# The mLSTM stabiliser as a prefix scan over rows of keys, one spread per head, and one branch product in another bank

## The reference, cut to what matters

```python
b = jnp.cumsum(fc, axis=-1)
log_d = jnp.where(causal, b[..., :, None] - b[..., None, :] + ic[..., None, :], -jnp.inf)
m_inter = b + m_prev[..., None]
m_t = jnp.maximum(m_inter, jnp.max(log_d, axis=-1))
a = jnp.exp(m_inter - m_t)
s_qk = jnp.einsum("bhtd,bhsd->bhts", qc, kc) * jnp.exp(log_d - m_t[..., None])
...
h = num / jnp.maximum(jnp.abs(den), jnp.exp(-m_t))[..., None]
...
mix = jax.nn.sigmoid(gm) * (y_m @ w_br_mlstm[l]) + jax.nn.sigmoid(gf) * (y_f @ w_br_fox[l])
```

## Time and profile before

| | us |
|---|---|
| median of 3 runs | 794.84 (794.53 to 795.08) |
| the profiled execution's own time | 794.99 |
| its span in the trace | 793.1 |
| TensorE busy | 778.2 (98%) |
| VectorE busy | 373.1 (47%) |
| ScalarE busy | 254.6 (32%) |
| GpSimd busy | 25.4 (3%) |

### The profile page before, as it was taken

One profiled execution on the slowest core, in us unless ns is written; L12 is line 12 of the kernel. 1 busy time (PEld: TensorE's weight loads), 2 busy tenths in 40 slices (PEclk: granted clock), 3 DMA queues, 4 the chain that ended last, 5 costly groups with the idle time before them and its releaser, 6 DMA issues.

```text
span 793.1 us, 9542 instructions
## 1 busy us (share of the span) xinstructions
PE 778.2 (98%) x3851; PEld 639.7 (81%) x3851; DVE 373.1 (47%) x576; ACT 254.6 (32%) x421; POOL 25.4 (3%) x45
## 2 busy tenths in 40 slices
PE   6999999999999999999999999999999999999996
PEld 6988888788666688888889888888888888888885
DVE  4688434356877444252446443343344444223224
ACT  6444221244455232322333322232233233123111
POOL 5000000012100000000000000000000000000000
PEclk9999999999999999999999999999999999999999
DMA  7434333211111035322421333233333223322302
GB/s 228 126 100 141 124 107 106 58 50 54 54 54 47 8 107 192 104 76 105 140 73 54 107 107 90 73 103 107 106 107 106 69 91 109 124 87 74 139 0 107
DMA packets 61916, 75.64 MB, mean 95 GB/s; under 512 B 3680, under 2 KB 49840, under 8 KB 61872
## 3 DMA queue, kind: packets, MB, share of 16 engines
q1 hardware_dynamic: 61872, 75.02, 29.5%
HBM read 72.92 MB, written 2.10 MB: 95 GB/s over the span
## 4 chain that ended last, share of the span: by engine, by line
PE 71%; issue 1%; DVE 0%; ACT 0%; POOLq 0%; POOL 0%; DVEq 0%; ACTq 0%
PE bank L1146 22%; PE bank L1148 22%; PE bank L1147 22%; PE bank L1367 1%; PE bank L1335 1%; PE bank L1352 1%; PE bank L1158 0%; PE bank L1342 0%; PE bank L1339 0%; ACT square_out L449 0%; DVE probs L978 0%; ACT x L684 0%; DVE yfT_lo L955 0%; DVE work L873 0%; DVE x L1118 0%
## 5 line engine op out<-in xcount | busy, mean ns | idle before, releaser
L1146 PE MATMUL bank<-hT_hi,w_hi 128*128 128x512 f32 (+1 forms) x680 | 261.2, 384 | 2.1 <-DVE hT_lo L709 2.1
L1148 PE MATMUL bank<-hT_hi,w_lo 128*128 128x512 f32 (+1 forms) x680 | 257.2, 378 | 0.0
L1147 PE MATMUL bank<-hT_lo,w_hi 128*128 128x512 f32 (+1 forms) x680 | 257.0, 378 | 0.0
L725 DVE TENSOR_TENSOR w_lo<-stage,w_hi 128x1024 fp32r<-128x1024 f32 x125 | 152.4, 1223 | 221.8 <-ACT w_hi L469 213.2
L469 ACT ACTIVATE w_hi<-stage 128x1024 fp32r<-128x1024 f32 x127 | 133.4, 1053 | 132.0 <-PE bank L1148 127.4
L1146 PEld LDWEIGHTS bank<-hT_hi,w_hi 128*128 128x128 f32 x680 | 128.8, 189 | 26.1 <-POOL w_lo L412 2.3
L1148 PEld LDWEIGHTS bank<-hT_hi,w_lo 128*128 128x128 f32 x680 | 128.7, 189 | 23.8
L1147 PEld LDWEIGHTS bank<-hT_lo,w_hi 128*128 128x128 f32 x680 | 128.8, 189 | 21.7
L1146 PE MATMUL bank<-w_hi,aT_hi 128*128 128x512 f32 x176 | 68.5, 389 | 0.0
L1147 PE MATMUL bank<-w_lo,aT_hi 128*128 128x512 f32 x176 | 68.5, 389 | 0.0
L1148 PE MATMUL bank<-w_hi,aT_lo 128*128 128x512 f32 x176 | 68.5, 389 | 0.0
(11 more groups left out here) (175 smaller groups left out, 765.3 us busy)
## 6 DMA issues: line engine op xcount, KB each, us to landing
stage<-in_w_in SPq DMA_DIRECT2D x21, 1024.0 KB, 5.2
stage<-in_w_gate SPq DMA_DIRECT2D x11, 1024.0 KB, 5.3
stage<-in_w_up SPq DMA_DIRECT2D x11, 1024.0 KB, 5.3
stage<-in_w_down SPq DMA_DIRECT2D x22, 512.0 KB, 4.4
stage<-in_w_out SPq DMA_DIRECT2D x4, 1024.0 KB, 5.0
x_nat<-in_x SPq DMA_DIRECT2D x4, 512.0 KB, 5.7
stage<-in_w_br_mlstm SPq DMA_DIRECT2D x4, 512.0 KB, 3.5
stage<-in_w_br_fox SPq DMA_DIRECT2D x4, 512.0 KB, 4.6
```

Of the source, the lines that this page charges most:

```text
L725: dve.tensor_tensor(ring(w_lo, g), staged(g), ring(w_hi, g).bitcast(F32), ALU.subtract).then_inc(lo_split, 1)
L1146: pe.matmul(o, a_hi, b_hi, start=first, stop=False)
L1147: pe.matmul(o, a_hi, b_lo, start=False, stop=False)
L1148: return pe.matmul(o, a_lo, b_hi, start=False, stop=last)
```

## The change

The four spreads of a key row per head are gone, with the maxima on them. In their place the running maximum is taken where the keys lie as rows: a `tensor_tensor_scan` on VectorE, for each block of queries q, over the (q + 1) x 128 keys of four heads on four partitions, straight from the bank of the transposes, with `before` of the head as start value. The scans run from q = 3 down to 0 and write the same row `m_rows` from its start, so that in the end each block of 128 columns is the one of its own q. For that, `ROW_CHUNKS` now puts all keys of q = 3 in bank 7, of q = 2 in bank 6, and of q = 0 and 1 in bank 5, and `before` is brought to rows by four matmuls with one column of the identity. ScalarE and VectorE write the high and low part as `m_both` (a buffer of 128x512 that GpSimd clears first). After the second granule of `G_FV`, four matmuls turn `m_rows` into columns for `m_floor`. The spread of a head is one fp32r matmul of 512 columns with `pick` as weights. The banks 5 to 7 are now free for the next taker when the scans have read them. The branch products of the mLSTM go to banks 2 and 3, those of FoX to banks 0 and 1.

```diff
+        m_both = at("m_both", [P, SEQ], F32R, R + 77 * K)
+        m_rows = work[0]
...
@@ POOL, among the constants
+            const(pool.memset(m_both[:, :].bitcast(F32), 0.0))
@@ ACT, in the loop over granules
+                if g == G_MV + 3:
+                    act.wait_ge(m_scan, ROWS)
+                    act.activation(m_both[0:H_M, :], m_rows[0:H_M, :], ACT.Copy).then_inc(m_hi_ready, 1)
...
-            act.wait_ge(m_step, 2)
+            act.wait_ge(m_step, 1)
@@ DVE, at g == G_MV + 2, behind the low halves of the keys
+                    dve.wait_ge(frame_T, 1)
+                    dve.tensor_copy(before_rows[:, :], psum[5][0:H_M, BEFORE_AT:BEFORE_AT + ROWS]).then_inc(before_copied, 1)
+                    dve.wait_ge(before_copied, 1)
+                    for i, q in enumerate(reversed(range(ROWS))):
+                        n = next(n for n, (a, b) in enumerate(ROW_CHUNKS) if a <= pair(q, 0) < b)
+                        c = (pair(q, 0) - ROW_CHUNKS[n][0]) * P
+                        if i >= 1:
+                            dve.wait_ge(m_scan, i)
+                        dve.tensor_tensor_scan(m_rows[0:H_M, 0:(q + 1) * P], psum[5 + n][0:H_M, c:c + (q + 1) * P],
+                                               before[0:H_M, 0, 0:1].to_broadcast([H_M, (q + 1) * P]),
+                                               before_rows[:, q:q + 1], ALU.max, ALU.add).then_inc(m_scan, 1)
+                if g == G_MV + 3:
+                    dve.wait_ge(m_hi_ready, 1)
+                    dve.tensor_tensor(m_both[LO:LO + H_M, :], m_rows[0:H_M, :], m_both[0:H_M, :].bitcast(F32),
+                                      ALU.subtract).then_inc(m_lo_ready, 1)
+                if g == G_FV + 2:
+                    dve.wait_ge(m_columns, 1)
+                    dve.tensor_tensor(m_floor[:, :, :], psum[M_COLUMNS_BANK][:, 0:ROWS * H_M].rearrange("p (q h) -> p q h", q=ROWS),
+                                      cum[:, :, 0:H_M], ALU.add).then_inc(m_step, 1)
...
-                if G_FQK <= g < G_MO:
-                    for u in spread_units(g - G_FQK):
-                        q, h = u // H_M, u % H_M
-                        dve.wait_ge(g_spread, u + 1)
-                        dve.reduce_max(m_stab[:, q, h:h + 1], psum[spread_bank(u)][:, 0:(q + 1) * P], AX.X).then_inc(g_max, 1)
...
@@ PE, keys_as_rows
-                    take(5 + n, (rows_lo_ready, n + 1))
+                    take(5 + n, (m_scan, (ROWS, 2, 1)[n]))
+                    if n == 0:
+                        for q in range(ROWS):
+                            pe.matmul(psum[5][0:H_M, BEFORE_AT + q:BEFORE_AT + q + 1], before[:, q, :], ident[:, 0:1],
+                                      start=True, stop=True)
...
+            def stabiliser_columns():
+                pe.wait_ge(m_scan, ROWS)
+                take(M_COLUMNS_BANK, (m_step, 1))
+                for q in range(ROWS):
+                    last = pe.matmul(psum[M_COLUMNS_BANK][:, q * H_M:(q + 1) * H_M], m_rows[0:H_M, q * P:(q + 1) * P],
+                                     ident[0:H_M, 0:H_M], start=True, stop=True)
+                last.then_inc(m_columns, 1)
...
-                for u in spread_units(b):
-                    q, h = u // H_M, u % H_M
-                    take(spread_bank(u), (g_max, u + 1))
-                    spread_row(spread_bank(u), h, q, True, True).then_inc(g_spread, 1)
@@ PE, mlstm_scores
-                    pe.wait_ge(m_step, 2)
+                    pe.wait_ge(m_lo_ready, 1)
...
-                for q in range(ROWS):
-                    last = pe.matmul(psum[2][:, q * P:(q + 1) * P],
-                                     m_stab[:, q, h:h + 1].to_broadcast([P, P]), ident[:, :], start=True, stop=True)
-                last.then_inc(m_spread, 1)
+                pe.matmul(psum[2][:, :], pick[:, h:h + 1].to_broadcast([P, P]), m_both[:, :], start=True,
+                          stop=True).then_inc(m_spread, 1)
@@ PE, the branches
-                    columns(g, 2 * j, (mix_step, 3 * b + 1), ymT_hi, ymT_lo, 0, KB, False)
+                    columns(g, YM_BANKS[j], (mix_step, 3 * b + 1), ymT_hi, ymT_lo, 0, KB, False)
...
-                    columns(g, 2 * j + 1, (mix_step, 3 * b + 2), yfT_hi, yfT_lo, KB, KB)
+                    columns(g, YF_BANKS[j], (mix_step, 3 * b + 2), yfT_hi, yfT_lo, KB, KB)
...
-ROW_CHUNKS = ((0, 4), (4, 8), (8, 10))
+ROW_CHUNKS = ((0, 3), (3, 6), (6, 10))
+BEFORE_AT = 3 * P
+M_COLUMNS_BANK = 4
+YM_BANKS, YF_BANKS = (2, 3), (0, 1)
```

More of the change, by code:

```diff
@@ L231, in block_kernel @@
         before = small("before", [P, ROWS, H_M])
-        m_stab = small("m_stab", [P, ROWS, H_M])
+        before_rows = small("before_rows", [H_M, ROWS])
         m_floor = small("m_floor", [P, ROWS, H_M])
@@ L268, in block_kernel @@
         rows_hi_ready, rows_lo_ready, rows_low_half = sem("rows_hi_ready"), sem("rows_lo_ready"), sem("rows_low_half")
-        g_spread, g_max, m_step, floor_ready = (sem(n) for n in ("g_spread", "g_max", "m_step", "floor_ready"))
+        before_copied, m_scan, m_hi_ready, m_lo_ready = (sem(n) for n in ("before_copied", "m_scan", "m_hi_ready", "m_lo_ready"))
+        m_columns, m_step, floor_ready = (sem(n) for n in ("m_columns", "m_step", "floor_ready"))
         m_spread, s_m, decay_exp, m_masked, weighted = (sem(n) for n in ("m_spread", "s_m", "decay_exp", "m_masked", "weighted"))
@@ L1042, in _ @@
                         s = mix_sum[b % 2]
-                        dve.scalar_tensor_tensor(out=s[:, :], in0=work[2 + j][:, :], scalar=1.0, in1=psum[2 * j][:, :],
+                        dve.scalar_tensor_tensor(out=s[:, :], in0=work[2 + j][:, :], scalar=1.0, in1=psum[YM_BANKS[j]][:, :],
                                                  op0=ALU.add, op1=ALU.mult).then_inc(mix_step, 1)
-                        dve.scalar_tensor_tensor(out=work[0][:, :], in0=work[4 + j][:, :], scalar=1.0, in1=psum[2 * j + 1][:, :],
+                        dve.scalar_tensor_tensor(out=work[0][:, :], in0=work[4 + j][:, :], scalar=1.0, in1=psum[YF_BANKS[j]][:, :],
                                                  op0=ALU.add, op1=ALU.mult).then_inc(mix_step, 1)
@@ L1263, in _ @@
                         keys_as_rows()
-            def spread_row(bank, lane, q, first, last):
-                n = (q + 1) * P
-                cols = slice(pair(q, 0) * P, pair(q, 0) * P + n)
-                both = pick[:, lane:lane + 1].to_broadcast([P, P])
-                pe.matmul(psum[bank][:, 0:n], both, rows_both[:, cols], start=first, stop=False)
-                return pe.matmul(psum[bank][:, q * P:n], ident_b[:, :], mask_b[:, :], start=False, stop=last)
+                    if n == 1 and d == 1:
+                        stabiliser_columns()
             for b in range(8):
                 z_columns(G_FQK + b, fqk_bank(b), (fq_ready, b + 1) if b < KB else (fk_ready, b - KB + 1))
-                if b == 0:
-                    pe.wait_ge(rows_lo_ready, 3)
-                for u in spread_units(b):
-                    q, h = u // H_M, u % H_M
-                    take(spread_bank(u), (g_max, u + 1))
-                    spread_row(spread_bank(u), h, q, True, True).then_inc(g_spread, 1)
             def mlstm_scores(h):
                 if h == 0:
-                    pe.wait_ge(m_step, 2)
+                    pe.wait_ge(m_lo_ready, 1)
                     pe.wait_ge(qk_ready, 8)
                 take(2, (decay_exp, 10 * (h + 1)))
-                for q in range(ROWS):
-                    last = pe.matmul(psum[2][:, q * P:(q + 1) * P],
-                                     m_stab[:, q, h:h + 1].to_broadcast([P, P]), ident[:, :], start=True, stop=True)
-                last.then_inc(m_spread, 1)
+                pe.matmul(psum[2][:, :], pick[:, h:h + 1].to_broadcast([P, P]), m_both[:, :], start=True,
+                          stop=True).then_inc(m_spread, 1)
                 for j in range(ROWS):
```

10 lines of the change are left out of this document (1 added, 9 removed).

## The result

| | before | after |
|---|---|---|
| median, same chip | 794.96 (794.53 to 795.39, 4 runs) | 788.50 (787.94 to 790.44, 4 runs) |
| the profiled execution / its span | 794.99 / 793.1 | 788.84 / 787.0 |

The ratio is 0.9921, with a 95% interval of 0.9909 to 0.9933. The forecast was 787.7 (785.9 to 789.9).

The account below looks back on a forecast made before the run. TensorE, busy 98% of the span, was taken to bound the kernel. Savings of 4.57 + 2.6 + 1.5 = 8.7 us less 1.6 added gave 7.1 off the median 794.84: 787.7 us, range 785.9 to 789.9.

Parts of the forecast that it names:

- Sixteen spreads: TensorE, projections of the FoX q and k: removing 16 spreads and their masks saves 4.57 us, all on the path.
- Small matmuls: TensorE: eight added float32 matmuls, for `before` as rows and the stabiliser's columns, cost 1.6 us together.
- The heads: TensorE, mLSTM heads: one fp32r matmul replaces four float32 spreads in each of four heads, saving 2.6 us.
- nothing new becomes late: Behind each head's spread: mask, exponentials and weighing start from the spread's end, so they add no wait.
- The bank: First branch product with `ymT`: in bank 2 it no longer waits for `yfT_lo`, and the 1.5 us goes whole.
- The scans, hidden: VectorE, after the keys' low halves: four scans, 1.6 us, cost nothing if they end by about 89.3 us.
- The memset, hidden: GpSimd at the start: one more memset of 512 columns, about 0.46 us, hidden by 0.1 us.
- The small matmuls at full price: Rival, TensorE's added matmuls: each record costs its whole length, 3.4 us instead of 1.6, 789.5 us; chance 0.13.
- free: Rival, TensorE's added matmuls: they slip under their neighbours and cost nothing, 786.1 us; chance 0.08.
- The branch's wait: Rival, branch products: the product with `yfT` waits after all or for weights, 1.5 us stays, 789.2 us; chance 0.06.
- The late scans: Rival, bank 5: slow scans make TensorE wait, slower than before from 15.6 us of scans; chance 0.02.
- The change does what it says: Its opposite was a rival, FoX projections: place, not removed matmuls, causes the 4.57 us; 2 us stays, 789.7 us; chance 0.01.

Follow-up runs that it names:

- e5: Changed kernel with the 16 spreads, masks and maxima put back, their results unused: 793.50 us, ratio 0.9976 to the kernel before.
- e6: Changed kernel with the stabiliser's columns made by four transposes instead of four float32 matmuls: 788.32 us, ratio 0.9913 to the kernel before.
- e1: Changed kernel with the next head's mask put ahead of the normalisation on VectorE: 787.56 us, ratio 0.9908 to the kernel before.
- e2: Kernel before with the next head's mask put ahead of the normalisation on VectorE: 795.31 us, ratio 1.000 to the kernel before.
- e4: Changed kernel with each head's stabiliser spread by four float32 matmuls from its columns again: 790.84 us, ratio 0.9948 to the kernel before.
- e3: Kernel before with only the branch products moved to the other banks: 793.74 us, ratio 0.9981 to the kernel before.
- e11: Changed kernel with two more memsets of 512 columns on GpSimd at the start: 789.11 us, one run.
- e7: Changed kernel with each of the four scans done three times: 792.52 us, ratio 0.9969 to the kernel before.
- e8: Changed kernel with early mask, columns by transposes, and head 3's normalising ahead of taking head 2's transposed output: 787.27 us, ratio 0.9901 to the kernel before.
- e9: Changed kernel run again without any edit: 789.11 us, ratio 0.9928 to the kernel before.

## Why the prediction was right, and the step that failed

- **Sixteen spreads, 4.57 us: right.** Shown by e5, 4.57 between two places of its trace. The way to it, the stretch less its projections by the pitch, counts the switches without naming them.
- **Small matmuls, 1.6 us: the sum right, its parts not.** Measured 0.37 for `before` (0.7 taken) and 1.19 for the columns (0.9 taken). The step that failed is one price of 0.085 for both, read off transposes. A record of `before` (four columns of weights, one moving) cost 0.27 / 8 = 0.034 us; one of the columns (128 columns of weights, four moving) cost 0.12, and e6 shows that a transpose of that shape costs 0.08. The errors of +0.3 and -0.3 cancelled, which is luck. The Trainium skill ("TensorE: Matmul & The Clock Gate", section "LDWEIGHTS (loading the stationary operand)") has the load go by the weights' columns alone. The estimate by it, 1.1 us, was closer for the columns than my 0.9, though 0.12 lies a little over its 0.107, and the 0.08 of the transposes below it; for `before` its 0.0 to 0.2 was too low by about as much as my 0.7 was too high.
- **The heads, 2.6 us: right where it was read, and wrong behind it.** By the first FoX logits 2.65 us had come. The failed step is "nothing new becomes late". I had argued that the mask hangs on the spread's end. It hangs on two things, and the other is VectorE's own turn: behind the gate and ScalarE's tanh for head 1, and behind the normalisation and GpSimd's power from then on. The change shortens neither by as much as TensorE's way: 0.03 to 0.37 us a head against 0.66 to 0.69. The trace before had it: head_output ended at 203.80, and the logits that need it started 0.16 us later. With the wait, after, they start 0.14 us behind its end (199.41 to 199.55). So that place had no slack at all. TensorE didn't show a wait there because it came at the same moment. e1, e2 and e4 show the mechanism from three sides: the earlier mask brings 1.2 us after and nothing before, and with slow spreads the wait goes.
- **The bank, 1.5 us: right.** 1.6 in the traces, and e3 alone gives 1.5. The slack of 1.3 us that was worked out for the product with `yfT` held: it starts at 267.51, `yfT_lo` ends at 266.10.
- **The scans, hidden: right, though they were priced at less than half.** Their size hardly mattered since the cover was read off first. The Trainium skill ("DVE: opcode table, instruction layouts, handler registers and perf-mode slots", section "6. Datapath and trigger behaviour") says half throughput for the built-in scan, and the estimate of 3 us by it was near. The trace after agrees: 2.08 ns an element (1.27 us for 512, 0.47 for 128), where the two-input operation that weighs the scores (L921), from PSUM too, takes 0.69 us for 512 elements and 0.28 for 128, 1.07 ns an element.
- **The memset, hidden: right.** 0.52 us, in the idle time that was there; e11 adds that the slack behind is real.
- **The rivals.** None came true. The small matmuls at full price (3.4 us) and free (0) both fall at 1.56. The branch's wait didn't come back. The late scans lost 0 and would begin to lose at 8 us, by e7. The change does what it says, by e5. None of them named VectorE's lag in the heads, which took 1.2 us, more than the error of any term that was priced. That the time lies in the range all the same is luck: the range was made wide for other cases, each worth 1.5 to 2 us, and the loss was smaller than they.

The sum of the terms as measured, 4.57 - 1.56 + 2.65 - 1.19 + 1.58 = 6.05, is the span's 6.1. The prediction's 8.7 - 1.6 lacked the fourth. The fourth is a reading from logits to logits, and e1 gives it back.

## What to carry to other kernels

A saving on the bounding engine inside a loop shortens its period, and what the other engines do between one turn and the next has to keep up: compare both periods before you count the saving in full, and look for handovers that arrive just in time, since an engine that comes at the same moment as its partner shows no wait and has no slack either. Where VectorE stands idle for another engine's result ahead of work that is ready, put that work in front, as long as nothing behind it gets short in turn (e8). An unpriced operation is best answered by the cover: how much time there is before someone needs it usually settles the case before its own cost does.

## What the runs showed of the hardware

- A float32 scan (`tensor_tensor_scan`) from PSUM takes 2.08 ns an element and about 0.2 us, with four partitions in use, twice the 1.07 ns of a plain two-input operation (L921).
- Small float32 matmuls of two shapes, two records each: 0.034 us a record with 128 rows by four columns of weights and one column moving, 0.12 with four rows by 128 columns and four moving. That the weights' columns make the difference is not shown by itself, since the other sizes differ too. As transposes, four records of 0.08 do what eight of 0.12 did.
- The start scatters: the same matmuls for `before` began between 77.07 and 77.97 us in the changed kernel and its variants. The rest doesn't, as far as two traces of one kernel can tell: the changed kernel's spans are 787.0 and 786.7 us (e9), `before` starts at 77.43 and 77.14, and from there to the end are 709.57 and 709.56. Slower executions, such as the 790.44 of the first measurement, have no trace. Differences inside a trace are steadier than differences of two spans.
